# A PEER encoder step on one Trainium2 core: the scratch of the dense weights laid out by expert row, then token, then column

## The reference

```
q = c @ w_q                                   # 8 heads, two halves of 128
top 16 of 128 keys in each half; top 16 of the 256 sums -> eidx = 128*i1 + i2, gate = softmax
act = gelu(einsum('td,tkd->tk', x, u[idx]))    # 128 experts of 16384 for each token
out = einsum('tk,tkd->td', gate * act, v[idx])
```

## Time and profile before

| | us |
|---|---|
| median of 3 runs | 3873.73 |
| lowest, highest | 3864.7, 3878.63 |
| the profiled execution's own time | 3875.81 |
| its span in the trace | 3874.0 |

### The profile page before, as it was taken

One profiled execution on the slowest core, in us unless ns is written; L12 is line 12 of the kernel. 1 busy time (PEld: TensorE's weight loads), 2 busy tenths in 40 slices (PEclk: granted clock), 3 DMA queues, 4 the chain that ended last, 5 costly groups with the idle time before them and its releaser, 6 DMA issues.

```text
span 3874.0 us, 27416 instructions
## 1 busy us (share of the span) xinstructions
PE 3162.0 (82%) x9486; PEld 1690.5 (44%) x9486; DVE 2752.2 (71%) x3853; ACT 686.1 (18%) x1653; POOL 1466.4 (38%) x905
## 2 busy tenths in 40 slices
PE   8998688999885459899878654699999999887927
PEld 4447333554374234355436644344444434343403
DVE  1006977667677778878757697878888999777772
ACT  1212110232010121023201266100000000011003
POOL 0001644545545434344334522332333334246560
PEclk9999799999998679999989856799999999998968
DMA  7889999999999999999999899999999999999995
GB/s 269 277 279 347 415 376 382 411 406 410 383 410 413 410 367 388 410 403 390 348 350 410 353 358 335 349 420 419 420 420 420 419 420 413 410 417 391 412 370 187
DMA packets 369923, 1470.90 MB, mean 380 GB/s; under 512 B 28152, under 2 KB 66488, under 8 KB 235576
## 3 DMA queue, kind: packets, MB, share of 16 engines
q0 software_dynamic: 129744, 944.82, 60.0%
q1 hardware_dynamic: 229392, 512.40, 35.5%
q10 hardware_dynamic: 10648, 11.92, 1.0%
HBM read 1443.36 MB, written 25.69 MB: 379 GB/s over the span
## 4 chain that ended last, share of the span: by engine, by line
DMA 39%; PE 31%; issue 13%; DVE 9%; POOL 4%; ACT 3%; ACTq 0%; SPq 0%; another core or an unknown queue 0%; DVEq 0%; POOLq 0%
PE psum L773 24%; DMA ring<-in_peer_v,eidx 18%; DMA W<-in_w_in 6%; DMA ring<-in_peer_u,eidx 4%; DMA W<-in_w_peer_q 4%; POOL ring L734 4%; DVE ring L2079 3%; DMA W<-in_w_out 3%; DVE arena L2091 2%; PE psum L1083 2%; DMA a_scratch<-W 2%; PE psum L1022 1%; DMA W<-in_w_ple_gate 1%; DMA a_scratch<-arena 1%; PE psum L1138 1%
## 5 line engine op out<-in xcount | busy, mean ns | idle before, releaser
L734 POOL DMA_INDIRECT ring<-in_peer_u,eidx x576 | 961.6, 1669 | 1654.8 <-DVE dots L2079 1208.7
L2079 DVE CUSTOM_DVE_ANT_0 ring<-ring,cx 128x2048 f32<-128x2048 f32 x576 | 1309.4, 2283 | 99.3 <-DMA ring<-in_peer_u,eidx 98.3
L773 PE MATMUL psum<-W,actT 128*128 128x512 f32 x2752 | 1237.5, 608 | 101.4 <-DMA W<-in_w_in 58.6
L773 PEld LDWEIGHTS psum<-W,actT 128*128 128x128 f32 x2752 | 530.7, 195 | 761.4 <-issue 668.0
L2091 DVE SCALAR_TENSOR_TENSOR arena<-ring,wts,arena 128x2048 f32<-128x2048 f32 x320 | 751.0, 2347 | 146.9 <-DMA ring<-in_peer_v,eidx 130.0
L734 POOL DMA_INDIRECT ring<-in_peer_v,eidx x320 | 501.5, 1567 | 637.8 <-DVE arena L2091 588.7
L1083 PE MATMUL psum<-arena 128*128 128x512 f32 x1024 | 448.2, 597 | 23.9 <-DVE arena L2002 23.9
L1083 PE MATMUL psum<-W,arena 128*128 128x512 f32 x1024 | 451.1, 599 | 17.4 <-DVE arena L2002 17.3
L773 PE MATMUL psum<-W,arena 128*128 128x512 f32 x768 | 347.8, 609 | 52.7 <-DMA W<-in_w_out 51.6
L1022 PE MATMUL psum<-actT,W 128*128 128x128 f32 (+2 forms) x1536 | 287.5, 352 | 71.0 <-DMA W<-in_w_peer_q 71.0
L1083 PEld LDWEIGHTS psum<-arena 128*128 128x128 f32 x1024 | 193.5, 191 | 268.1 <-issue 236.2
(11 more groups left out here) (279 smaller groups left out, 2013.0 us busy)
## 6 DMA issues: line engine op xcount, KB each, us to landing
W<-in_w_in SPq DMA_DIRECT2D x168, 1024.0 KB, 13.9
W<-in_peer_v SPq DMA_DIRECT2D x64, 1024.0 KB, 15.1
arena<-in_peer_v SPq DMA_DIRECT2D x64, 1024.0 KB, 17.3
W<-in_w_out SPq DMA_DIRECT2D x48, 1024.0 KB, 14.4
W<-in_w_peer_q SPq DMA_DIRECT2D x48, 1024.0 KB, 25.2
W<-in_w_ple_gate SPq DMA_DIRECT2D x48, 1024.0 KB, 16.2
actT<-a_scratch SPq DMA_DIRECT2D x64, 256.0 KB, 26.7
ring<-in_peer_u,eidx POOLq DMA_INDIRECT x576, 12.7
```

The lines of the kernel that those rows point to most:

```text
L734: pool.indirect_dma_start(ring[:, slot, :], None, a["peer_u" if what == "u" else "peer_v"][0], off(ix, 0)).then_inc(ring_in[slot], 16)
L773: ins = pe.matmul(bank(4 * s + j), lhs(k, j), W[:, k, :], start=(k == 0), stop=(k == KT - 1))
L2079: dve.tensor_tensor_reduce(row, row, cx[:, :], 1.0, 0.0, ALU.mult, ALU.add, dots[:, n % DEEP, c:c + 1]).then_inc(u_used, 1)
```

## The change

The scratch has the shape (expert row i, token, column k) instead of (token, expert). The write of a batch then puts, for each i, four tokens' 128 columns side by side: 2048 contiguous bytes instead of four runs of 512. The read of a chunk takes, for each token, four runs of 512 bytes, one for each i, where it took 2048 contiguous bytes. The bytes, the number of DMAs, the waits and the order on every engine stay as they are.

```diff
-        a_keep = nc.dram_tensor("a_scratch", (TOKENS, NKEY * NKEY), F32, kind="Internal").ap()
+        a_keep = nc.dram_tensor("a_scratch", (NKEY, TOKENS, NKEY), F32, kind="Internal").ap()
...
-                sp.dma_start(a_keep[b * BATCH:(b + 1) * BATCH, :].rearrange("t (i k) -> i t k", i=NKEY),
+                sp.dma_start(a_keep[:, b * BATCH:(b + 1) * BATCH, :],
                              a_stage(b).rearrange("p (t k) -> p t k", t=BATCH)).then_inc(a_out[b % 4], 16)
...
-                        sp.dma_start(a_chunk(c)[:, b, :], a_keep[b * P:(b + 1) * P, c * CHUNK * NKEY:(c + 1) * CHUNK * NKEY]
+                        sp.dma_start(a_chunk(c)[:, b, :].rearrange("t (i k) -> t i k", i=CHUNK),
+                                     a_keep[c * CHUNK:(c + 1) * CHUNK, b * P:(b + 1) * P, :].rearrange("i t k -> t i k")
                                      ).then_inc(chunk_in[c % 2], 16)
```

## The result

The changed kernel takes 3960.21 us (median of 6 runs, 3949.43 to 3967.36) against 3871.59 us before (6 runs): a ratio of 1.023, 95% interval 1.0208 to 1.0253. It is slower by some 89 us, where "no change", 3878, was forecast, and it lies outside the range of 3853 to 3925.

What follows compares the result with a forecast made beforehand. The kernel was taken as DMA-bound. Against the profiled 3875.81 us, build -19, dense stage +27 and tail -5 gave +3, 3879; the median being 2.1 us lower, 3878 was stated, range 3853 to 3925.

Steps and rivals of the forecast that it cites:

- Turns: Both DMA queues: while both have work they alternate packet by packet, so a 512 B packet behind busy q0 costs 0.34 us.
- price of a packet: DMA engine time for each packet: 26.4 ns for 512 B, 87 ns for 2 KB, 315 ns for 8 KB.
- first rival: Faster, 3859 us: dense stage pays for its work alone, by early gaps in q0 or many 512 B packets per turn; chance 0.22.
- Build: Stage before the dense one, writing the scratch: 7, 7 and 10 us gained, 5 lost on first chunk reads, -19 us in all.
- first half: First half of the build: writes stop falling behind and DVE's waits go, 7 us gained, bounds 0 and 7.3.
- pitch of 128 KB: Third rival, build writes: 2 KB runs 128 KB apart in HBM are slow to land, 3927 us; chance 0.05.
- Dense stage: Stage reading the chunks: each step goes from 31.27 to 32.2 us as chunks land late, +27 us over 30 steps.
- prediction's own loop: Dense stage: tiles are issued when PE ends a step, so the period is (28.7 + L) / 2, 29.9 us before the change.
- L: Dense stage: time from issue of a chunk's tiles to the chunk's use, 31.0 us before, 34.8 forecast after.
- high end: Dense stage: the gap comes too late, another pair of gathers goes first, L = 40.2, period 34.5 us, +96 us.
- Tail: After the dense stage: the gather ring is ahead by up to four gathers, 10 us of DMA work; half counted, 5 us gained.
- second rival: Slower, dense stage: q0's gap comes too late, chunks wait for another pair of gathers, 3895 to 3946 us; chance 0.22.

## Why the prediction was wrong

- **Turns: right; price of a packet: a little low.** By the trace a late chunk took 16 to 23 us beside q0, 21.9 was reckoned. The 512 B reads took 29.4 ns in the mean, not the 26.4 of the writes, so the work in 29 steps grew by 13 us for chunks where 9 were counted for 30. Equal counts say that neither queue gets more turns than the other; whether the packets go one by one or in equal bursts they do not say, and by the count the price is the same either way. What they speak against is the first rival's many small packets for one large one.
- **Build: right in sum.** -19 forecast, -19.8 at tiles 2, -23.5 in the kernel with the writes alone. By the dates of SP's issues the first half gave 3 us and the second 10, where 7 and 7 were forecast, the end 10.6 for 10, and the first chunks took 3.1 us more for 5. That the halves' errors cancel is luck. The pitch of 128 KB did no harm.
- **Dense stage: wrong, and this is the step.** "By hand: when the tiles are through, about 3.4 gathers, 27 packets an engine, still come in turns ... the period 31.8". I looked for one steady step and gave it one chunk, of 10.2 us, between the busy q0 and the empty one. The runs show no such step: in the pair shown, chunks take 21.9 and 3.6 us in turn. After a late chunk the ring is full and q0 dry, so the next is early, but an early chunk gives nothing back, since a step can't be shorter than PE's 28.3 us; the late one costs 12 to 21 us in full. The mean of the chunk times, 12.0 us, is near the 10.2 that I took. The mean of the steps is not, 35.1 against 32.2. The prediction's own loop, two steps in 28.7 + L, holds if L is the late chunk's: L was 2706.34 - 2660.22 = 46.1 us, which with 3 us for the clock makes 77.8, and the pair took 77.7. The high end had L at 40.2 at most.
- **"The DMA engines never idle" (first rival's support) was wrong for the same reason.** It holds while one of the queues has work. SP issues tiles when PE ends a step, and the chunk right behind; once both have landed early, q1 is empty until PE is done, and a full ring, with DVE blocked on PE, empties q0 too. This is some 67 us of the 112; the other 45 are the packet time of above, of which the prediction had 9.
- **Not counted: the clock.** Behind each long stall it stood at its lower level, 1.4 to 3 us for a long step, some 28 us of the 112.
- **Tail: right in kind, too small.** The ring was ahead by the end, by 471 packets or nearly four gathers, and DVE hardly waited for gathers in the stage. What comes behind the stage was 17.5 us shorter, where 5 were forecast and 10 allowed. Why it was more than the ten stays open. The gain hides that the stage lost 128.8 us to its end and not 112.
- The second rival had the right sign and the right place, a chunk that waits in turns for more gathers than the step allows. Its price, +45 to +96 in the stage, was short of what the stage lost, again because it was worked out for equal steps.

## What to carry to other kernels

When a transfer is cut into smaller packets, count its packets on an engine times the packet of the busiest other queue, and not its bytes; if that exceeds the lead that the transfer has, try another step of lead first. Test a "steady" step for stability: where a late arrival costs in full and an early one returns nothing, a mean of late and early is no forecast. Then look for what runs dry. Steps that alternate lost nothing here as long as the DMA engines had work; what cost was a stall that left them idle. Here, moving the small packets from the stage that writes to the stage that reads cost 2.3%, and nothing once the reading side had a step in hand.

## What the runs showed of the hardware

- The turns between q0 and q1 go by the number of packets and not by size, also where only SBUF's side of a transfer is cut (the reads alone: +105.6 us with nothing changed in HBM).
- A 512 B write packet took 26.4 ns and a 512 B read packet 29.4 ns in the mean of the changed kernel's dense stage. 1024 read packets passed nearly alone in 2.4 to 4.3 us on 16 engines.
- Behind each wait of PE of 8.9 to 17.8 us the next turn, eight matmuls, took 1.97 us instead of 1.04 to 1.09, at a granted clock of 0.50 (thirteen waits in the changed kernel).
- Issuing can take SP long. In the changed kernel it once needed 10.73 us for two chunk DMAs, where 0.9 us was usual before, and in the kernel with the chunk one step earlier 13.66 us for four tiles. No run shows why. For chunks and tiles, issues of over 5 us came only in kernels with chunk reads in 512 B packets on SP's queue:

```profile
2615.50 10.73 SPq L677 DMA_DIRECT2D actT<-a_scratch  x2
```
